# PEER layer: dense expert products with unsplit fp32 weights, and 64 instead of 48 tokens served by row fetches

## What is computed

```python
def peer_ffn(xn, w_peer_q, sub_keys, expert_u, expert_v):
    ...
    sv, si = lax.top_k(s, PEER_TOPK)
    ...
    best, pick = lax.top_k(cand, PEER_TOPK)
    expert_idx = jnp.take_along_axis(cand_idx, pick, axis=-1)
    gates = jax.nn.softmax(best, axis=-1)
    ...
    def step(args):
        xc, ic, gc = args
        u = expert_u[ic]
        hval = jnp.einsum('cd,chkd->chk', xc, u).astype(jnp.float32)
        a = (gc * jax.nn.gelu(hval, approximate=False)).astype(xc.dtype)
        return jnp.einsum('chk,chkd->cd', a, expert_v[ic])
```

## Time and profile before

| | |
|---|---|
| median of 3 runs | 1311.26 us (1310.68 to 1311.98) |
| profiled execution, its own time | 1311.49 us |
| its span, first to last instruction | 1309.7 us |
| busy share PE, PEld, DVE, ACT, POOL | 99%, 92%, 82%, 63%, 17% |
| granted TensorE clock, mean | 0.999 |
| DMA | 292.74 MB, mean 224 GB/s |
| V stage | 288.0 us for 120 units |

### The profile page before, as it was taken

How to read it: one execution, slowest core, us unless ns; L and a number is a source line. 1 busy time by engine, 2 the same in 40 slices (tenths; PEclk the granted TensorE clock), 3 DMA queues, 4 the chain that set the end, 5 groups by cost and what they waited for, 6 DMA issues and landing times.

```text
span 1309.7 us, 21763 instructions
## 1 busy us (share of the span) xinstructions
PE 1294.8 (99%) x8061; PEld 1199.0 (92%) x8061; DVE 1068.7 (82%) x1974; ACT 820.4 (63%) x1601; POOL 220.7 (17%) x163
## 2 busy tenths in 40 slices
PE   8999999999999999999999999999999999999998
PEld 6998888888889888888999999999999999999996
DVE  6968776666678656769999989999999989998985
ACT  6886465555556555454666888888765555555553
POOL 3001130000000000000100021110234336544410
PEclk9999999999999999999999999999999999999999
DMA  6533366555445344654666666556799999999972
GB/s 228 178 124 126 113 226 193 191 190 185 160 159 177 129 145 150 235 200 150 211 207 222 207 214 207 196 204 214 270 346 323 367 356 346 363 366 352 342 278 89
DMA packets 82784, 292.74 MB, mean 224 GB/s; under 512 B 10397, under 2 KB 11053, under 8 KB 82422
## 3 DMA queue, kind: packets, MB, share of 16 engines
q1 hardware_dynamic: 68182, 239.65, 52.8%
q0 software_dynamic: 14496, 51.69, 10.9%
HBM read 288.95 MB, written 2.34 MB: 222 GB/s over the span
## 4 chain that ended last, share of the span: by engine, by line
PE 86%; DVE 7%; ACT 3%; issue 2%; DMA 1%; SPq 0%; POOL 0%; POOLq 0%; DVEq 0%; ACTq 0%
PE bank L2408 84%; DVE wl L665 2%; PE bank L2506 1%; ACT wh L1745 1%; DMA raw<-in_wts 1%; PE bank L2494 1%; DVE oi L1580 1%; DVE rows L1603 1%; DVE gates L1635 1%; DVE oj L1576 0%; ACT oi L2328 0%; ACT oi L2332 0%; DVE gates L1588 0%; ACT kdz L1751 0%; DVE St L855 0%
## 5 line engine op out<-in xcount | busy, mean ns | idle before, releaser
L2408 PE MATMUL bank<-hTb,wh 128*128 128x416 f32 (+3 forms) x2768 | 823.8, 363 | 1.5 <-DVE wl L665 1.3
L2408 PE MATMUL bank<-hTb,wl 128*128 128x208 f32 (+2 forms) x2584 | 651.8, 264 | 0.0
L665 DVE TENSOR_TENSOR wl<-raw,wh 128x1024 fp32r<-128x1024 f32 x429 | 523.1, 1226 | 128.7 <-ACT wh L1745 126.9
L1745 ACT ACTIVATE wh<-raw 128x1024 fp32r<-128x1024 f32 x429 | 449.0, 1055 | 203.4 <-PE bank L2408 132.4
L2408 PEld LDWEIGHTS bank<-hTb,wh 128*128 128x128 f32 (+1 forms) x2768 | 504.3, 188 | 22.2 <-issue 2.9
L2408 PEld LDWEIGHTS bank<-hTb,wl 128*128 128x128 f32 (+1 forms) x2584 | 491.5, 190 | 4.8
L2408 PE MATMUL bank<-wh,hTb 128*128 128x512 f32 (+2 forms) x552 | 175.6, 400 | 1.7 <-DVE hTb L699 1.7
L2408 PEld LDWEIGHTS bank<-wh,hTb 128*128 128x128 f32 (+1 forms) x552 | 102.4, 187 | 24.6 <-DVE wl L665 1.8
L645 POOL DMA_INDIRECT rows<-in_v_rows,pick x48 | 97.4, 2029 | 98.3 <-DVE acc L1614 85.7
L645 POOL DMA_INDIRECT rows<-in_u_rows,pick x48 | 70.6, 1471 | 229.7 <-DVE dots L1603 227.5
L2408 PE MATMUL bank<-wl,hTb 128*128 128x512 f32 (+2 forms) x276 | 100.7, 390 | 0.0
(11 more groups left out here) (429 smaller groups left out, 1396.1 us busy)
## 6 DMA issues: line engine op xcount, KB each, us to landing
raw<-in_wts SPq DMA_DIRECT2D x441, 512.0 KB
x<-in_x SPq DMA_DIRECT2D x4, 256.0 KB, 6.9
sk<-in_sk SPq DMA_DIRECT2D x1, 1024.0 KB, 7.3
spill<-x SPq DMA_DIRECT2D x1, 1024.0 KB
x<-spill SPq DMA_DIRECT2D x4, 256.0 KB
rows<-in_u_rows,pick POOLq DMA_INDIRECT x48
rows<-in_v_rows,pick POOLq DMA_INDIRECT x48
gb<-in_g_ffn SPq DMA_DIRECT2D x1, 512.0 KB
```

The costliest lines, as they stand in the source:

```text
L665: e.tensor_tensor(b[:, :], raw[u % RAW][:, :], a[:, :].bitcast(F), ALU.subtract).then_inc(S("lo"), 1)
L1745: e.activation(parts_of(u)[0][:, :], raw[u % RAW][:, :], ACT.Copy).then_inc(S("hi"), 1)
L2408: return e.matmul(o, l, r, start=first, stop=last, skip_group_check=True)
```

## The change

1. `WHOLE` names all 128 U units. They are not split any more: PE multiplies `raw` as it lies, as fp32, by `xt` (high plus low half of the activations added up by POOL, fp32), eight matmuls of TN columns per unit. `high`, `low`, `low_half`, `ones` and `summed` skip the U units, and SP refills a raw buffer when PE has finished the unit ("done") instead of when `low` has.
2. `MORE` 16 -> 32: 64 tokens take the sparse way (64 + 64 slots), TN = 192 the dense way, NC = 48.
3. `NP` 50 -> 36, `NB` 5 -> 3 (the memory of the other two one-hot pairs is now `xt`), and DVE makes `oi` for every third chunk instead of every second, ACT the others.
4. The slot tables: 68 slots in the U stage (one behind each of units 45..84, then two behind every three units), 60 in the V stage.
5. Counts, and the places at which ACT makes key copies and the softmax exponentials during the selection, move with NP.

```diff
-NP, NB = 50, 5
+NP, NB = 36, 3
 AHEAD = 2
-MORE = 16
+MORE = 32
...
+WHOLE = tuple(range(NE))
...
+        xt = sb("xt", [128, 8, TN], F, XO)
...
-            at = {GATED - 1 - 3 * k: SOON - 1 - k for k in range(SOON)}
-            for n in range(GATED, NE - 2, 2):
-                at[n] = len(at)
+            at = {NP + 9 + k: k for k in range(NC - 8)}
+            for n in range(GATED, NE - 1):
+                if (n - GATED) % 3 < 2:
+                    at[n] = len(at)
...
                     if u >= RAW:
-                        e.wait_ge(S("lo"), u - RAW + 1)
+                        if u - RAW in whole_units:
+                            e.wait_ge(S("done"), u - RAW + 1)
+                        else:
+                            e.wait_ge(S("lo"), nth_split(u - RAW))
...
             copied(I["few_x"], h5[128 - FEW:128, 1, :])
+            e.wait_ge(S("hT_lo"), 24)
+            e.wait_ge(S("in_end"), 16)
+            e.tensor_tensor(xt[:, :, :], hTh[:, :, 0:TN].bitcast(F), hTl[:, :, 0:TN].bitcast(F),
+                            ALU.add).then_inc(S("hT_lo"), 1)
...
             def low(n):
                 for u in range(lows[0], min(n + 1, len(units))):
-                    e.wait_ge(S("hi"), u + 1)
+                    if u in whole_units:
+                        continue
+                    e.wait_ge(S("hi"), nth_split(u))
...
-                if c % 2 == 0:
+                if on_vector(c):
...
             def high(n):
                 for u in range(highs[0], min(n + 1, len(units))):
+                    if u in whole_units:
+                        continue
...
-                if not added(n):
-                    e.wait_ge(S("gelu"), n - 1)
-                copy((low_half if added(n) else us)[n % 2][:, :], B[2 + n % 4][:, TN:2 * TN]).then_inc(S("u_out"), 1)
+                if n not in WHOLE:
+                    if not added(n):
+                        e.wait_ge(S("gelu"), n - 1)
+                    copy((low_half if added(n) else us)[n % 2][:, :], B[2 + n % 4][:, TN:2 * TN]).then_inc(S("u_out"), 1)
...
-            at_keys = {20: (0, 0, 0), 21: (0, 0, 1), 23: (0, 1, 0), 25: (0, 1, 1),
-                       36: (1, 0, 0), 37: (1, 0, 1), 38: (1, 1, 0), 39: (1, 1, 1)}
+            at_keys = {15: (0, 0, 0), 16: (0, 0, 1), 17: (0, 1, 0), 18: (0, 1, 1),
+                       27: (1, 0, 0), 28: (1, 0, 1), 29: (1, 1, 0), 30: (1, 1, 1)}
...
-                if n == 41:
+                if n == 32:
...
+            def unit_whole(unit, bank):
+
+                n = nth(*unit)
+                assert n == started[0], (unit, units[started[0]])
+                started[0] += 1
+                e.wait_ge(S(f"raw{n % RAW}"), 16 * (n // RAW + 1))
+                e.wait_ge(S("hT_lo"), 25)
+                for k in range(8):
+                    t = mm(bank[:, 0:TN], raw[n % RAW][:, two(128, k)], xt[:, k, :], k == 0, k == 7)
+                t.then_inc(S("done"), 1)
...
-                unit_M(("U", ORDER[n]), B[2 + n % 4], width=TN)
+                if n in WHOLE:
+                    unit_whole(("U", ORDER[n]), B[2 + n % 4])
+                else:
+                    unit_M(("U", ORDER[n]), B[2 + n % 4], width=TN)
```

More of the change, by code:

```diff
@@ L351, in program, with nth_split, split_of @@
         Q0 = nth("T", "w_peer_q_2", 0, 512, 0)
+        U0 = nth("U", ORDER[0])
+        whole_units = tuple(U0 + n for n in WHOLE)
+        def nth_split(u):
+            return u + 1 - sum(w <= u for w in whole_units)
+        def split_of(n):
+            return min(n, NE - 1) + 1 - sum(w <= n for w in WHOLE)
         def parts_of(u):
@@ L389, in nth_sum, with on_vector, nth_on @@
                 return n - 3
-            return 13 + n - nth_added(n)
+            return 12 + split_of(n) + max(0, n - NE + 1) - nth_added(n)
+        def on_vector(c):
+            return c % 3 == 0
+        def nth_on(vector, c):
+            return sum(on_vector(i) == vector for i in range(c + 1))
         def added(n):
-            return n < SUMMED or n < GATED and n % 2 == 0
+            return n not in WHOLE and (n < SUMMED or n < GATED and n % 2 == 0)
         def nth_added(n):
@@ L2266, in gelu @@
                     e.wait_ge(S("u_add"), nth_added(n))
-                else:
+                elif n not in WHOLE:
                     e.wait_ge(S("u_sum"), nth_sum("U", n))
@@ L2347, in scalar, with factors @@
                 copy(gates[:, 0:NE - n, two(4, c)], v[:, 0:NE - n, :]).then_inc(S("G_out"), 1)
-            after_dots = {j: n for n, j in slots_taken()[1].items()}[SLOTS - 1] + 1
+            at_u, at_v = slots_taken()
+            after_dots = {j: n + 1 for n, j in at_v.items()}.get(SLOTS - 1, -1)
+            after_dots_u = {j: n + 1 for n, j in at_u.items()}.get(SLOTS - 1, -1)
+            def factors():
+                e.wait_ge(S("used"), used_by(SLOTS - 1))
+                e.activation(factor[:, :], dots[:, :], ACT.Gelu).then_inc(S("used"), 1)
             def high_of(n):
@@ L2381, in scalar @@
                 if n == after_dots:
-                    e.wait_ge(S("used"), used_by(SLOTS - 1))
-                    e.activation(factor[:, :], dots[:, :], ACT.Gelu).then_inc(S("used"), 1)
+                    factors()
                 if n == DENSE:
@@ L3176, in tensor @@
                 part_V(held[n], n, (0, 1, 2, 3))
-            e.wait_ge(S("u_sum"), nth_sum("U", NE - 1))
+            e.wait_ge(S("gelu"), NE)
             for n in range(2):
```

28 lines of the change are left out of this document (15 added, 13 removed).

## The result

| | before | changed |
|---|---|---|
| median | 1310.98 us (20 runs, 1309.66 to 1313.74) | 1314.73 us (20 runs, 1309.81 to 1317.48) |
| ratio | | 1.0026, 95% interval 1.002 to 1.0033 |
| profiled execution, and its span | 1311.49, 1309.7 | 1309.81, 1308.1 |
| U stage (first U matmul to first V matmul) | 368.7 | 379.1 |
| V stage | 288.0 | 277.5 |

The changed kernel is slower by 3.7 us in the median, and its runs spread over 7.7 us where those of the kernel before spread over 4.1. The profiled execution happened to be its fastest. Single runs that took half as long again or more (2599 us once in e2, 2090 and 3229 us once each in the kernel before) are left out of all medians and ranges.

What follows compares the result with a forecast made beforehand. PE was taken to bound the kernel, busy 99% of the span. U +8.8, V -12.5 and the U to V hand-over +1.5 sum to -2.2 us from the median 1311.26, giving 1309.0 us; range 1301 to 1317.

Steps and rivals of the forecast that it cites:

- U records: U units on PE: an fp32 record of 192 columns takes 0.162 us (0.160 to 0.163), a unit 2.59 us.
- Chunk period: PE's time in the U stage for one unit with a chunk's products: 3.48 us.
- Selection: In U ahead of the chunks: must be complete after 36 units, nothing to spare, 0.5 us charged.
- ACT and xt hidden: ACT's 3.0 us one-hot chunks fit PE's 3.48 us period; POOL's 5.4 us for `xt` is covered by the query units.
- V pair: V stage: going from 416 + 208 to 384 + 192 columns cuts a pair from 0.300 to 0.287 us, -12.5 us.
- the floor: V pairs: a matmul with new weights doesn't go below about 0.105 us, so only the wide matmul shrinks.
- The rival that these pairs have no such floor: V stage: the pair takes 0.280 us, 6.7 us more saved, 1302 us; chance 0.16.
- Waits of V: U to V hand-over: the second V unit's halves and ACT's last gelu come late, +1.5 us (0 to 5).
- Transfers bind: Last 43 U units: landing times from 7.8 us on set the period; 1319 us at 8.4, 1314 at 8.0; chance 0.24.
- What would show it: Signs in the profile: first V matmul at 996 to 998 us, units of 3.48 us in chunks, V units 2.30 apart.
- The sign that I had named for transfers: Forecast right on transfers if PE has no wait for raw in U and under 3 us at the first V units.
- theory B: From the experiments, not the prediction: the spread of the runs comes from elsewhere than V's weights, the stages always costing the same.

Runs made afterwards that it cites:

- e2: The changed kernel with the last 8 U units split again; median 1311.1 us, ratio to before 1.0006.
- e3: The changed kernel with the last 43 U units (behind the chunks) split again; median 1305.2 us, ratio to before 0.9963.
- e14: The changed kernel with the last 20 U units split again; median 1310.0 us, ratio to before 0.9992.
- e8: The changed kernel with 14 slots moved from the U units behind the chunks into V; median 1320.2 us, ratio to before 1.007.
- e4: The changed kernel with narrow row fetches (64 of 1024 columns) for all 60 slots in V; median 1307.8 us, ratio to before 0.9976.
- e9: e3 plus narrow row fetches (64 of 1024 columns) in V; median 1305.5 us, ratio to before 0.9967.
- e10: The kernel before with narrow row fetches (64 of 1024 columns) in V; median 1310.6 us, ratio to before 1.0001.
- e13: The changed kernel with narrow row fetches for only the first 8 of V's 60 slots; median 1311.5 us, ratio to before 1.0007.
- e6: The kernel before with 64 sparse tokens instead of 48, all weights still split; median 1355.6 us, ratio to before 1.0338.
- e7: e3 with every third of the 43 U units left unsplit; median 1316.1 us, ratio to before 1.0038.
- e12: The changed kernel with narrow row fetches only in the 43 U units behind the chunks; median 1310.5 us, ratio to before 1.0002.
- e15: The changed kernel with the two matmuls of each V pair swapped from the third expert on; median 1313.6 us, ratio to before 1.0026.
- e16: e3 with slots laid earlier (66 instead of 68 in U) and V's pair order swapped as in e15; median 1302.6 us, ratio to before 0.9945.

## Why the prediction failed

The forecast was 1309.0 us, the median is 1314.7: inside the range, but on the other side of no change. By its own steps:

- *U records*: 0.1625 us, 2.60 per unit, at the upper bound (0.163), not the 0.162 taken: +1.2 us over 2048 records. Chunk period 3.50 (I had 3.48). Selection 0.20 us (0.5). U stage +10.4 (forecast +8.8). The four passes of the Trainium skill (FP8 and Floating Point Precision, TensorE Precision Notes) agree with these records too.
- *ACT and xt hidden*: right. ACT has 109 of 170 us in the chunks, `xt` took 3.49 us (I had 5.4) well ahead of U.
- *V pair*: the floor was wrong. Its reason, that no matmul with new weights goes below 0.105 us, came from fp32 products of 64 columns; the `wl` matmul of 192 columns takes 0.087 us with new weights before each. Both matmuls shrank, the pair to 0.2845, between my 0.287 and the rival's 0.280: -14.9 us, where I had -12.5. The Trainium skill's P / 1.2 ns for a load (TensorE: Matmul & The Clock Gate, LDWEIGHTS), 107 ns, is not what limits these pairs. e3's trace agrees with the figure itself: the two loads of a pair start 0.108 and 0.176 us apart by turns, and together they leave room in 0.2845 us. The rival that these pairs have no such floor had the direction right, took 0.280, and like the forecast assumed one pace where there are two.
- *Waits of V*: **the step that failed**. I had 1.5 us (0 to 5). It is the term that I put at the hand-over alone. With the pair's measured price the profiled run pays 4.4 in V (0.8 in its first 15 us, 2.2 in late starts behind them, 1.4 in the slower pace, which no term of mine had). The median run is 4.9 us longer than the profiled one and presumably pays about as much again; that is inferred, from e14's 9.2 and e2's 10.8 us. By the sum of the profiled run, +10.4 of U, -10.5 of V and -1.5 elsewhere (the stage starts 1.35 us earlier), the change is worth -1.6 us; -2.2 was forecast. What I forecast was a run with little lost, as the fastest are.
- *The reason of the failure*: I wrote that V's transfers stay at 349 GB/s, so that nothing changes in V but the first units. The rate did stay. What went was the lead. I had seen that the unsplit units take away four buffers of depth, and charged this at the hand-over alone, as if V could catch up; with 350 of the 360 to 370 GB/s that these traces show at best (370 over 50 us in the kernel before, 366 over 200 us in e8), it can't.
- *Transfers bind* (the rival that came true in its number, 1314 to 1319): it had the right resource in the wrong stage. It put the loss in the U units behind the chunks, at a landing time above 7.8 us. PE had no wait for `raw` there; the loss was in V. That the number fits is luck.
- *What would show it*: the first V matmul at 997.01, 3.50 in the chunks, no wait for `raw` in U, all as written, and still the median came out on the other side. The sign that I had named for transfers, under 3 us of waits at the first V units, held as well. One profile of one run could not have shown it; the spread of the runs did.

What is shown: V pays for transfers when it starts without a lead (e3, e4, e9, e10, e13's profile), at the edge of what the DMA engines deliver (e6, e8); late starts cost their own length, and stretches at half clock (e2, e7, e8) and the slower pace (e12, e13, the changed kernel) set in at some of them. What stays open: none of the changed kernel's runs above 1314 us was profiled, so how its median divides between waits and pace is inferred from its variants; what spreads e4's and e9's runs over more than 5 us without V's row traffic, which is as much as is left of theory B; and what in a late start decides which pace follows.

## What to carry to other kernels

A transfer rate that doesn't change is no proof that transfers are still hidden: count for each stage how many loads stand ready when it starts, and whether the stage can rebuild that lead at its own rate. Here giving up the split buffers in the last 43 of 128 units removed a lead that V could not rebuild. Splitting those units again gained 9 us, 5 of them by U's own shorter units and the rest behind it. Where runs of a kernel spread more than those of the kernel before, one profile, above all one from the low end, does not show the cost; look for what late starts trigger, and check the distance between starts, since a busy engine at full clock can still have two paces.

## What the runs showed of the hardware

- The same alternation of matmuls (384 columns with one set of weights, 192 with the next) runs at 0.2845 or at 0.2900 us per pair, at full clock and without idle time. The slower pace set in only at a late start; it ended at one, but for e15 at 1106.1 us and e2 at 1187.0 us. With 416 and 208 columns only 0.300 was seen (the kernel before, e10).
- With the two swapped the slower pace held for 827 and 936 of 960 pairs in the two profiles there are (e15, e16); with the old order for more than half of them in one of 14.
- In e7 waits of PE of 0.35 us (997.79), 1.51 us (1000.66) and 0.20 us (1003.27) came with some 6.5 us of pairs at half pace, at a granted clock of 0.50 from 1002 to 1006 us. The changed kernel's profiled run, with waits of 0.5 and 0.6 us, had none.
- A matmul of 192 columns with new fp32r weights took 0.087 us while the loads of a pair started 0.108 and 0.176 us apart (e3), an fp32 record of 192 columns 0.1625 us, three quarters of the 0.216 for 256 and half a ns more.
- Over 200 us of V the DMA engines gave at most 366 GB/s (e8), 362 with PE undisturbed (e3); in e6 PE waited at 353.
